# Light experts in float32 by two 64-column operands side by side, in units of 1792 columns

## What is computed

```python
def swiglu(x, wg, wu, wd):
    return (jax.nn.silu(x @ wg) * (x @ wu)) @ wd

def moe_swiglu(x, w_router, we_gate, we_up, we_down):
    logits = (x @ w_router).astype(jnp.float32)
    top_vals, top_idx = lax.top_k(logits, TOP_K)
    gates = jax.nn.softmax(top_vals, axis=-1)
    ...
    for e in range(N_EXPERTS):
        out = out + combine[..., e:e + 1] * swiglu(x, we_gate[e], we_up[e], we_down[e])
```

## Time and profile before

| | |
|---|---|
| median of 3 runs | 1278.1 us (1277.04 to 1278.29) |
| span of the profiled execution | 1276.0 us |
| PE, DVE, ACT busy | 96%, 87%, 73% of the span |
| HBM read | 428.40 MB, 340 GB/s over the span |
| moved by the DMA queues | 434.49 MB |

### The profile page before, as it was taken

The page is one execution under the profiler, slowest core; times in us unless marked ns, Lnnn a source line. Parts: engine busy times, 40 slices in busy tenths (PEclk is TensorE's granted clock), DMA queues, the critical chain, the costliest instruction groups (busy, mean ns, idle before and its releaser), DMA issues.

```text
span 1276.0 us, 15815 instructions
## 1 busy us (share of the span) xinstructions
PE 1227.3 (96%) x6181; PEld 1053.5 (83%) x6181; DVE 1106.1 (87%) x861; ACT 933.7 (73%) x716; POOL 39.8 (3%) x57
## 2 busy tenths in 40 slices
PE   9999999999999999999999999999999999999886
PEld 8988888888989888888887877888787888887664
DVE  6978555568889999999999999999999899999887
ACT  5575444445868787888888888887988888788774
POOL 0100000001010000000000000000000000000100
PEclk9999999999999999999999999999999999999998
DMA  9947555537459999999999999999999999999993
GB/s 317 346 163 262 190 182 192 198 110 254 159 171 348 370 410 399 398 412 411 409 409 401 411 409 412 411 394 408 411 410 410 412 405 408 411 411 404 412 411 159
DMA packets 143556, 434.49 MB, mean 341 GB/s; under 512 B 8964, under 2 KB 50996, under 8 KB 131188
## 3 DMA queue, kind: packets, MB, share of 16 engines
q1 hardware_dynamic: 139936, 421.07, 85.8%
q0 software_dynamic: 3456, 12.32, 2.8%
q10 hardware_dynamic: 84, 0.02, 0.0%
HBM read 428.40 MB, written 4.98 MB: 340 GB/s over the span
## 4 chain that ended last, share of the span: by engine, by line
PE 61%; DVE 17%; DMA 15%; ACT 5%; issue 2%; SPq 0%; ACTq 0%; DVEq 0%
DVE w_lo L1032 14%; DMA raw<-in_we_down 8%; PE turn L1686 7%; PE turn L1688 7%; PE turn L1687 7%; PE accp L1686 5%; PE accp L1687 5%; PE accp L1688 5%; DMA raw<-in_we_gate 5%; PE turn L1798 4%; PE turn L1795 4%; ACT w_hi L669 4%; PE turn L1797 2%; PE turn L1796 2%; DMA raw<-in_we_up 2%
## 5 line engine op out<-in xcount | busy, mean ns | idle before, releaser
L1032 DVE TENSOR_TENSOR w_lo<-raw,w_hi 128x1792 fp32r<-128x1792 f32 (+3 forms) x447 | 895.8, 2039 | 96.8 <-ACT w_hi L669 91.5
L669 ACT CAST w_hi<-raw 128x1792 fp32r<-128x1792 f32 (+2 forms) x441 | 756.0, 1724 | 173.9 <-PE turn L1688 43.2
L2130 PE MATMUL turn<-w_hi,t_both 128*128 128x448 f32 x512 | 193.8, 379 | 16.0 <-DVE w_lo L1032 15.4
L2131 PE MATMUL turn<-w_lo,t_both 128*128 128x448 f32 x512 | 188.7, 369 | 0.0
L1686 PE MATMUL turn<-w_hi,a_hi 128*128 128x448 f32 x496 | 184.0, 371 | 0.0
L1688 PE MATMUL turn<-w_hi,a_lo 128*128 128x448 f32 x496 | 181.7, 366 | 0.0
L1687 PE MATMUL turn<-w_lo,a_hi 128*128 128x448 f32 x496 | 181.7, 366 | 0.0
L2130 PEld LDWEIGHTS turn<-w_hi,t_both 128*128 128x128 f32 x512 | 97.5, 190 | 36.6 <-issue 20.0
L2131 PEld LDWEIGHTS turn<-w_lo,t_both 128*128 128x128 f32 x512 | 97.4, 190 | 7.9 <-issue 0.2
L1686 PEld LDWEIGHTS turn<-w_hi,a_hi 128*128 128x128 f32 x496 | 93.1, 188 | 9.8
L1687 PEld LDWEIGHTS turn<-w_lo,a_hi 128*128 128x128 f32 x496 | 93.2, 188 | 8.4
(11 more groups left out here) (298 smaller groups left out, 1529.8 us busy)
## 6 DMA issues: line engine op xcount, KB each, us to landing
raw<-in_we_gate SPq DMA_DIRECT2D x128, 896.0 KB, 8.6
raw<-in_we_up SPq DMA_DIRECT2D x128, 896.0 KB, 9.2
raw<-in_we_down SPq DMA_DIRECT2D x96, 1024.0 KB, 9.6
raw<-in_w_in SPq DMA_DIRECT2D x18, 1024.0 KB, 9.0
raw<-in_we_down SPq DMA_DIRECT2D x32, 512.0 KB, 8.6
raw<-in_w_down SPq DMA_DIRECT2D x11, 1024.0 KB, 5.1
raw<-in_w_gate SPq DMA_DIRECT2D x10, 1024.0 KB, 5.3
raw<-in_w_up SPq DMA_DIRECT2D x10, 1024.0 KB, 5.4
```

Source lines behind the costliest of these rows:

```text
L669: nc.scalar.copy(w_hi[:, p % PARTS, 0:filled(p)], raw[:, p % RING, 0:filled(p)]).then_inc(hi_done, 1)
L1032: return nc.vector.tensor_tensor(out, whole, hi.bitcast(f32), ALU.subtract)
L2130: nc.tensor.matmul(to[:, c, :], few, wh[:, kk, c, :], start=(k == 0), stop=False)
L2131: last = nc.tensor.matmul(to[:, c, :], few, wl[:, kk, c, :], start=False, stop=(k == KD - 1))
```

## The change

Light experts are no longer split. All their pieces are in `WHOLE`: SP reuses the slot of a light piece after TensorE has used it. Their tokens lie once, in float32 (`x_few`, 64 columns). A light unit has 1792 columns, so there are eight light units instead of sixteen, with eight gate, eight up and eight down pieces each. A gate or up piece is 128 rows by 1792 columns, one stretch of 7,168 bytes a partition. For each 128 rows and each part of 448 columns two matmuls follow each other: one writes PSUM rows 0 to 63 with columns of the first 896, the other rows 64 to 127 with columns of the second 896. Down blocks go in the same way, with output columns 0 to 511 in rows 0 to 63 and 512 to 1023 in rows 64 to 127. `raise_low`, `few_low` and the adding of the two row halves are gone. The order becomes "HHH", "LHH" six times, "H", "LL". In a light unit behind a heavy one the four down pieces come after all eight up pieces. The end has one copy and four float32 matmuls of 64 rows each.

```diff
-    ORDER = "HHH" + "LH" * 12 + "H" + "L" * QUARTERS
+    ORDER = "HHH" + "LHH" * 6 + "H" + "LL"
+    N_UNITS = len(ORDER)
+    UNITS_OF = {"H": 4, "L": 2}
+    ROWS_PIECES = {"H": 4, "L": 8}
...
     def mixed(i):
-        return "uuuu" if i == 0 else "uuuudddd" if i == N_UNITS - 1 else "uduududd" if light(i) else "uduuuddd"
+        if i == 0:
+            return "uuuu"
+        if i == N_UNITS - 1:
+            return "uuduuduudduuddd" + "d"
+        if light(i):
+            return "uuuuuuuudddd" if not light(i - 1) else "uduududuuduuddd" + "d"
+        return "uduuuddd" if not light(i - 1) else "uduuuddddddd"
...
-    WHOLE = {PLACE[piece] for piece in (("down", N_UNITS - 3, 1), ("down", N_UNITS - 2, 2))}
+    WHOLE = {PLACE[piece] for piece in PLACE if light(piece[1])}
...
+                w = we_gate if which == "gate" else we_up
+                if light(i):
+                    load(PLACE[which, i, pair],
+                         expert_rows(w, ORDER[i], k)[:, pair:pair + 1, 2 * s * WIDE:2 * (s + 1) * WIDE])
...
+            def keep_last():
+
+                used(MOE_AT + MOE_PIECES - 1)
                 act.wait_ge(acc_added, added(ALL_ROWS))
-                nc.scalar.copy(last_half_rows, last_sum(LAST[1])).then_inc(last_ys_hi, 1)
+                nc.scalar.copy(last_rows_in, few_sum).then_inc(last_kept, 1)
...
             def times_up(i):
                 dve.wait_ge(e_silu, i + 1)
...
+                used(last_up(i))
+                nc.vector.tensor_tensor(parts(h_e[:]), up_banks, parts(silu_e[:, i % 2, :]), ALU.mult).then_inc(e_h, 1)
...
+            def few_down(i, pair):
 
                 _, s = expert_step(i)
+                half, quarter = divmod(pair, 4)
                 w = unsplit(down_piece(i, pair)).rearrange("p (j d) -> p j d", d=D)
...
+                hT = (hT_last if i == N_UNITS - 1 else hT_few[:]).rearrange("p (b h t) -> p b h t", h=2, t=FEW)
+                for j, block in enumerate(blocks_of(quarter)):
+                    for rows, cols in zip(HALVES, LAST):
+                        last = nc.tensor.matmul(few_sum[rows, :], hT[:, block, half, :], w[:, j, cols],
+                                                start=(s == 0 and pair == 0 and block == 0),
+                                                stop=(s == 1 and pair == 7 and block == BLOCKS - 1))
                 last.then_inc(piece_used, 1)
...
+            def few_rows(i, which, k):
...
+                w = unsplit((up_piece if which else gate_piece)(i, k)).rearrange("p (h c f) -> p h c f", h=2, c=2)
+                for c in range(2):
+                    for h, rows in enumerate(HALVES):
+                        last = nc.tensor.matmul(to[rows, c, :], x_few[:, e % 2, k, :], w[:, h, c, :],
                                                 start=(k == 0), stop=(k == KD - 1))
                 last.then_inc(piece_used, 1)
```

More of the change, by code:

```diff
@@ L439, in last_bank, with rows_written @@
             return turn[:, 2 * n + (cols.start == BANK), :cols.stop - cols.start]
-        def last_sum(cols):
-            half, at = divmod(cols.start, BANK)
-            return accp[:, 2 + half, at:at + cols.stop - cols.start]
+        def rows_written(j):
+            return 16 * sum(2 if kind == "L" else 1 for kind, _ in KEPT[:j])
         token_rows_in = [ys_rows[:], more_rows[:]]
@@ L2148, in last_down @@
[L2148 to L2164 removed]
+                    turned_left(i)
@@ L2166, in last_scatter @@
+                    if s == 0 and e:
+                        pe.wait_ge(ys_kept, KEPT.index((kind, e - 1)) + 1)
+                if light(i):
+                    few_down(i, pair)
+                else:
+                    down_pair(pair, split(down_piece(i, pair)), s == 0, s == 3).then_inc(piece_used, 1)
             def last_scatter():
                 pe.wait_ge(slots_read, 1)
-                pe.wait_ge(last_ys, 1)
+                pe.wait_ge(last_kept, 1)
                 for n in range(NT):
-                    for part in (ys_hi, ys_lo):
-                        last = nc.tensor.matmul(last_bank(n, LAST[0]), pickT[:, 1, n * P:(n + 1) * P], part[:, LAST[0]],
-                                                start=(part is ys_hi), stop=(part is ys_lo))
-                    last.then_inc(scattered, 1)
@@ L2175, in last_scatter @@
-                pe.wait_ge(last_ys_hi, 2)
-                for n in range(NT):
-                    nc.tensor.matmul(last_bank(n, LAST[1]), pickT[:, 1, n * P:(n + 1) * P].bitcast(f32), last_half_rows,
-                                     start=True, stop=True).then_inc(scattered, 1)
+                    for rows, cols in zip(HALVES, LAST):
+                        nc.tensor.matmul(last_bank(n, cols), pickT[rows, 1, n * P:(n + 1) * P].bitcast(f32),
+                                         last_rows_in[rows, :], start=True, stop=True).then_inc(scattered, 1)
@@ L2289, in _ @@
                 pairs = {"u": 0, "d": 0}
-                kinds = mixed(i)
-                for place, c in enumerate(kinds):
+                for c in mixed(i):
                     if c == "u":
@@ L2300, in _ @@
                     pairs[c] += 1
-                    if light(i) and place == 1:
-                        add_low(i, 0)
-                    if light(i) and place == kinds.rindex("u") + 1:
-                        add_low(i, 1)
-            last_down()
+            for pair in range(8):
+                down(N_UNITS - 1, pair)
             last_scatter()
```

318 lines of the change are left out of this document (100 added, 218 removed).

## The result

| | before | after |
|---|---|---|
| median | 1277.65 us (1277.04 to 1278.29, 4 runs) | 1318.19 us (1317.33 to 1321.42, 4 runs) |
| span of the profiled execution | 1276.0 us | 1315.5 us |
| PE, DVE, ACT busy | 1227.3, 1106.1, 933.7 us | 1205.1, 715.7, 585.6 us |
| mean granted clock of TensorE | 0.994 | 0.972 |

The ratio is 1.0322, with a 95% interval of 1.0308 to 1.0337: slower by 40.5 us, where 1268 us, 10 us faster, was forecast. All three computing engines have less to do, DVE by 390 us, and the kernel is slower by 3%.

A forecast was written before the change was run, and what follows sets the result against it. Transfers were taken as the bound, PE and DVE close behind. -9.0 + 2.0 + 2.6 + 1.0 - 6.6 = -10.0 us on a span of 1276.0, with 2.1 us carried along, gave 1268 us; range 1258 to 1310.

The forecast's parts named there:

- What is put in their place: the slots: Expert stage: light pieces hold raw slots until PE uses them; seams cost +2.0, +2.6 and +1.0 us, bounds 0 and +12.
- The first seam: First light pieces after three PE-bound heavy units: the bus idles 1.5 to 2 us, priced at +2.0 us.
- A faster byte: Light gate and up loads: one stretch of 7,168 bytes moves at 418 instead of 405 GB/s, -9.0 us.
- the place and not the length: Light gate and up loads: rate depends on place, so bytes are no faster; 1279 us, no change, chance 0.15.
- TensorE in a light unit: Light units' matmuls take 37 us side by side, 73 in sequence; 37 taken, PE sum 790 us, term zero.
- Side by side: Light units: two 64-column operands in different array columns run at once, 37 us a unit.
- one after the other: Rival, light units: the two operands do not overlap, 73 us a unit, PE bounds; 1472 us, chance 0.12.
- partial overlap: Rival, light units: two matmuls take 1/1.4 of twice one, 52.4 us a unit; 1308 us, chance 0.12.
- Splits taken away: 190 light pieces no longer cost DVE 380 us, nor ACT its cast; covered by the transfers, 0 us.
- The end: After the last landing: no split, PE follows each landing, first add after 3.3 us; -6.6 us, bounds -4 and -8.
- The clock: Rival, light units: TensorE's clock falls; 4 us cost 2, hidden by slack; low throughout gives 1472 us, chance 0.03.

The follow-up runs named there:

- experiment eight: Changed kernel with light gate and up pieces loaded as two stretches of 3,584 bytes instead of one of 7,168: six slots 1319.47 us, eight slots 1274.47 us.
- experiment four: Changed kernel, six slots, with small dummy float32 matmuls filling TensorE's waits at two kinds of seam: 1295.22 us, ratio 1.0138.

## Why the prediction was wrong, point by point

**The step that failed is "What is put in their place: the slots".** It said that a first slot comes back after 5.4 us plus PE's lag, that a lag up to 5.6 us costs nothing, and that a second heavy unit adds 3.9 us of it, so that all seams together cost 2.0 + 2.6 + 1.0 = 5.6 us, at most 12. The last landing came 45.5 us later although the byte was worth 9.9 us (experiment eight): the seams cost 55.4 us, 54 by the record of landings. (The 9.9 us are counted as eaten by the seams, since with six slots the longer stretches brought nothing.)

The mechanism was named and the threshold held; the lag was wrong. The record of landings gives it for each of the seven light units behind a heavy one: from the landing of the last heavy piece to the end of the first light block, less 5.4 us, it is 9.0, 8.8, 5.0, 7.6, 7.0, 7.5 and 10.1 us. Only the 5.0 is under 5.6, and there alone the seventh light piece lands the usual 2.2 us behind the sixth; at the others it is 3.9 to 6.7 us. What was missed are two terms of the lag. One is TensorE's waits for splits that light work no longer covers, 5.11 and 3.83 us in the group shown; the other is the matmuls at 1.2 GHz behind them (experiment four: 1.9 to 5.0 us a group). TensorE makes good a part of this in the light unit, so the lag is less than their sum with the 3.9.

A whole kind of seam was put at nothing as well: the light down pieces, which the first heavy unit behind a light one has to fetch while TensorE is busy with heavy ones (the dip at 516 us). Summed over the landings, each interval less the piece's own time on the bus, the changed kernel lost 47.9 us more than the one with eight slots: 22.8 in the light units, 16.8 in the first and 8.3 in the second heavy unit behind them. So the seams that were priced are about half of it. A lag that "stays just under" a threshold deserved to be priced from both sides of it; I priced only the near one. With eight slots (4.4 us more that are free, 10.0 in all) the lags are 14.1 us at the first seam and 4.3 to 9.1 at the others, and come to nearly no loss: with the last landing at about 1246.5 us, the seams of that kernel cost 1246.5 - 1253.6 + 9.9 = 2.8 us.

**The first seam: right.** +2.0 us was said; the bus is at a share of 0.69 in 455 to 461 us of the kernel after and 0.64 with eight slots, 1.9 and 2.2 us.

**A faster byte: right in mechanism and size.** -9.0 us was said, 9.9 measured once the bus is the bound, nothing with six slots. The bounds allowed that the place and not the length made the rate; experiment eight settles it for the length. The Trainium skill's rule for a packet's fixed cost (DMA: Bandwidth & Descriptors, "Why small descriptors are slow (HBM only)") gave an estimated -3.8 us: it has the sign, and less than half of the size of the 9.9.

**TensorE in a light unit: right.** Side by side was said, 37 us. Neighbouring weight loads come in pairs, the next pair 0.375 us later. Timeline of the kernel after, PE's loads:

```profile
458.75 0.14 PEld L2012 LDWEIGHTS turn<-raw,x_few 128*64 128x64 f32 x2 [0.23 <-issue]
459.13 0.14 PEld L2012 LDWEIGHTS turn<-raw,x_few 128*64 128x64 f32 x2 [0.23 <-issue]
```

Eight records of a piece take 1.72 us. The rivals "one after the other" (1472 us) and "partial overlap" (1308 us) are false, though the latter lies nearest to the result: a time that fits is not a mechanism. The rule that loads overlap matmuls only across row groups (the Trainium skill, TensorE: Matmul & The Clock Gate, "The mechanism") would, taken alone, have forbidden this pairing, since both operands use all 128 rows; the trace speaks against it for two operands in different columns. The same section also lets a load go ahead into a background weight buffer, and no run here tells which of the two is at work.

The sum of TensorE's work, 790 us, had no term for waits or clock, and its conclusion ("this term is zero") does not hold: with 57.4 us of waits for splits and 32.4 us lost at 1.2 GHz on top it is an estimated 880 us, as long as the 875 us that the transfers had. Nothing was left to absorb a lag.

**Splits taken away: right.** DVE lost 390 us (380 said), ACT 348, and this bought nothing by itself. What the prediction did not draw from it: ACT and DVE fell idle and TensorE fast, so that the split's latency, hidden before, came to lie on TensorE's path. "Covered by the transfers: 0 us" was a statement on throughput, and a latency took its place.

**The end: right.** -6.6 us was said, -6.0 measured; from the last landing to the first add 4.7 us (3.3 said), before 9.9. By the record of landings it is 3.6 us against 7.6, and the end gained 4.8: still inside the bounds of -4 to -8, but the 9.9 of the prediction began where the bytes grew thin, 2.2 us before the last piece had landed.

**The clock: the rival was real, with the wrong place and price.** It was looked for inside the light units, where TensorE is busy part of the time; there it stays at 1.00. It falls after the waits of 4 to 5 us at the seams, and "hidden by 15 us of slack in a unit" was wrong because the lateness there is passed on to the slots. It lost TensorE 32.4 us and the kernel 23.

**The sum with the failed step mended.** With what was measured for each term, six slots give -9.9 + 55.4 - 6.0 = +39.5 us, the difference of the spans (1315.5 - 1276.0). Eight slots give -9.9 + 2.8 - 6.0 = -13.1 us, where the prediction's own terms gave -10.0. Both agree by construction, as the seams are what the other terms leave.

**What stays open.** The steps of 34.4 and 19.2 us are read as seams covered one after the other, and no experiment took a single seam away. Light units of 896 columns left unsplit in the old order were not tried, nor the kernel before with eight slots, whose place `t_both` takes; its bus idles only 2.1 us, so little could come of them there. Why the bus moves 313 GB/s at a share of 0.98 behind the first dip was not looked into.

## What to carry to other kernels

When a buffer is handed from an early consumer (here a split) to a late one (here TensorE), count the lag of the late consumer at each change of the kind of work: all the waits that it takes there, the clock after them, and the work queued ahead of it, and set that against the transfers that the ring holds. Work removed from idle helpers frees no time, but the memory that it leaves can: the change was a loss of 3.2% with six slots and a gain of 1.0% with two slots more in the space that its own packed tokens had left. And test a suspected cause both with the resource short and with it plentiful: order, clock and slots each seemed to be worth 16, 23 and 54 us, and these were largely the same microseconds.

## What the runs showed of the hardware that was not expected

What the prediction took without a row is now shown: two float32 operands of 64 columns each overlap fully, with 0.19 us a record of 448 columns, where the earlier trace rows give 0.43 x 448 / 512 = 0.375 for records one after the other, and this holds also where four records of one half follow each other in the program (12.30 us for 64). The granted clock falls behind a wait of about 5 us (0.72 in 489 to 495 us after a wait of 5.11), and then a matmul takes 0.63 instead of 0.39 us; filled with small matmuls, the same wait leaves the clock at 1.00. Stretches of 7,168 instead of 3,584 bytes are worth 2.7 to 2.9% of the bus' rate (422 and 425 against 411 and 413 GB/s).
